# The final norm taken by halves of a row, its root's table loaded behind the sigmoids, and its output rows written from another queue

## The reference, cut to what matters

```
    gate = jax.nn.sigmoid(rms_norm(x, norm_ple) @ w_ple_gate)
    x = x + gate * (pemb @ w_ple_proj)
    ...
    y_prompt = rms_norm(x_p, final_norm)
    y_sample = rms_norm(x_s, final_norm)

def rms_norm(x, gain):
    xf = xf * lax.rsqrt(jnp.mean(xf * xf, axis=-1, keepdims=True) + EPS)
    return (xf * gain.astype(jnp.float32)).astype(x.dtype)
```

## Time and profile before

| what | value |
|---|---|
| median of three runs | 1063.93 us (1061.81 to 1066.5) |
| profiled execution, its own time | 1061.5 us |
| its span (first to last instruction) | 1059.9 us |
| mean granted TensorE clock | 0.992 of full |
| PE busy | 1030.5 us, 97% of the span |
| DVE, ACT, POOL busy | 300.5, 243.0, 91.5 us |
| DMA, mean over the span | 273 GB/s |

### The profile page before, as it was taken

The page is one execution under the profiler, slowest core; times in us unless marked ns, Lnnn a source line. Parts: engine busy times, 40 slices in busy tenths (PEclk is TensorE's granted clock), DMA queues, the critical chain, the costliest instruction groups (busy, mean ns, idle before and its releaser), DMA issues.

```text
span 1059.9 us, 14325 instructions
## 1 busy us (share of the span) xinstructions
PE 1030.5 (97%) x5734; PEld 524.7 (50%) x5734; DVE 300.5 (28%) x798; ACT 243.0 (23%) x503; POOL 91.5 (9%) x133
## 2 busy tenths in 40 slices
PE   7999999999999999999999999999999999999994
PEld 4468777455666667775543333333333333333342
DVE  2134222655333323121441111111111111132252
ACT  2021211456222242000231411111111111111153
POOL 0020040000232220000000000000000000000100
PEclk9999999999999999999999999999999999999998
DMA  9980496100655688363399999999999999999921
GB/s 324 262 240 2 157 165 195 53 29 1 185 167 165 215 282 224 152 238 119 124 369 396 376 426 426 426 426 430 427 429 426 428 428 426 427 428 425 377 78 32
DMA packets 58359, 288.93 MB, mean 273 GB/s; under 512 B 10211, under 2 KB 14540, under 8 KB 45566
## 3 DMA queue, kind: packets, MB, share of 16 engines
q1 hardware_dynamic: 48414, 259.61, 63.2%
q0 software_dynamic: 9648, 28.43, 9.6%
q10 hardware_dynamic: 240, 0.09, 0.0%
HBM read 277.87 MB, written 19.55 MB: 281 GB/s over the span
## 4 chain that ended last, share of the span: by engine, by line
PE 54%; DMA 8%; DVE 1%; issue 1%; ACT 0%; POOL 0%; SPq 0%; DVEq 0%; POOLq 0%
PE ps L1207 19%; PE ps L608 9%; PE ps L1235 9%; DMA reg_k<-in_w_exp_up_dram 7%; PE ps L1179 4%; PE ps L1104 3%; PE ps L679 2%; PE ps L1192 1%; PE ps L1183 1%; DMA late<-y_rows 1%; PE ps L1223 1%; PE ps L627 1%; PE ps L1075 1%; PE ps L686 1%; DVE x L2285 0%
## 5 line engine op out<-in xcount | busy, mean ns | idle before, releaser
L1207 PE MATMUL ps<-ring,reg_xh 128*64 128x512 f32 x512 | 148.7, 595 | 2.3 <-DMA ring<-in_w_exp_up_dram 0.9
L1207 PE MATMUL ps<-late,reg_xh 128*64 128x512 f32 x336 | 148.6, 595 | 0.7 <-DMA reg_k<-in_w_exp_up_dram 0.7
L1207 PEld LDWEIGHTS ps<-ring,reg_xh 128*64 128x64 f32 x512 | 46.2, 137 | 86.7 <-issue 84.2
L2252 DVE TENSOR_TENSOR reg_xh<-reg_xh,ps 64x512 f32<-64x512 f32 x32 | 22.1, 692 | 230.0 <-ACT reg_xh L1619 230.0
L1619 ACT ACTIVATE reg_xh<-ps 64x512 f32<-64x512 f32 x32 | 34.0, 1064 | 213.5 <-PE ps L1207 213.5
L1207 PE MATMUL ps<-reg_k,reg_xh 128*64 128x512 f32 x176 | 77.8, 595 | 0.0
L2471 POOL DMA_INDIRECT y_rows<-reg_xh,slot_row x29 | 28.3, 976 | 544.3 <-ACT reg_xh L1630 503.3
L917 PE MATMUL ps<-reg_xh,ring 128*128 128x320 f32 x256 | 73.5, 436 | 0.0
L1207 PEld LDWEIGHTS ps<-late,reg_xh 128*64 128x64 f32 x336 | 44.4, 137 | 45.3 <-issue 44.7
L608 PE MATMUL ps<-reg_xh,ring 128*128 128x320 f32 x224 | 60.9, 433 | 0.0
L1179 PE MATMUL ps<-reg_xh 128*64 128x512 f32 x256 | 60.5, 592 | 0.0
(11 more groups left out here) (425 smaller groups left out, 1374.4 us busy)
## 6 DMA issues: line engine op xcount, KB each, us to landing
ring<-in_w_exp_gate_dram SPq DMA_DIRECT2D x21, 2048.0 KB, 19.2
ring<-in_w_in_dram SPq DMA_DIRECT2D x12, 2048.0 KB, 10.5
ring<-in_w_exp_down_dram SPq DMA_DIRECT2D x11, 2048.0 KB, 23.9
ring<-in_w_exp_up_dram SPq DMA_DIRECT2D x11, 2048.0 KB, 23.7
late<-in_w_exp_gate_dram SPq DMA_DIRECT2D x10, 2048.0 KB, 19.8
reg_k<-in_w_exp_up_dram SPq DMA_DIRECT2D x10, 2048.0 KB, 24.2
late<-in_w_exp_up_dram SPq DMA_DIRECT2D x10, 2048.0 KB, 23.2
reg_xh<-in_w_exp_down_dram SPq DMA_DIRECT2D x10, 2048.0 KB, 23.4
```

The lines of the kernel that those rows point to most:

```text
L1207: last = pe.matmul(out[64 * part:64 * part + 64, :], xb[:, k, :], ws_[part][:, k, :], start=(k == 0), stop=(k == KT - 1))
L2252: dve.tensor_tensor(sg.rearrange("p (m q) -> p m q", m=4), sg.rearrange("p (m q) -> p m q", m=4), ps[64:128, 2 + par, :].rearrange("p (q m ...
```

## The change

It does four things.

1. ACT executes a root of a number nobody needs (`stat[:, 1, 1, t]`) right behind the sigmoids of each tile, and then takes the squares in two halves of 512, each of which waits for its half of `x` alone. The two sums go to two columns of `stat`.
2. DVE adds the two sums with two small instructions and, between them, multiplies `x` with `gain_f` by halves into `ysb` (`gained`). After the reciprocal, one `tensor_scalar` multiplies the 1024 channels of `ysb` by it, in place.
3. The three transfers of output rows are issued by SP and no longer by POOL. SP waits for `normalised` ahead of each.
4. The copy of window rows is counted by a semaphore that it shares with the gates' transfers (`gate_out` gets a new name), POOL waits for it inside the block, and `out_done` counts the three output transfers alone (48).

```diff
@@ block.sync, behind the branch
+            for t in range(2):
+                sp.wait_ge(normalised, t + 1)
+                sp.dma_start(y_prompt[0, 128 * t:128 * t + 128, :], ysb[:, t, :]).then_inc(out_done, 16)
+            sp.wait_ge(normalised, 3)
+            sp.dma_start(y_sample.rearrange("a b n -> (a b) n"), ysb[0:64, 2, :]).then_inc(out_done, 16)
@@ block.scalar, for each tile behind its sigmoids
-                act.wait_ge(y_done, 2 * t + 2)
-                act.activation(ysb[0:rows, t, :], x[0:rows, t, :], ACT.Square,
-                               accum_out=stat[0:rows, 4, 0, t:t + 1]).then_inc(sq_done, 1)
+                link(act.activation(stat[:, 4, 2, t:t + 1], stat[:, 1, 1, t:t + 1], ACT.Sqrt))
+                for c in range(2):
+                    act.wait_ge(y_done, 4 * t + c + 1)
+                    act.activation(xn2[0:rows, t, 512 * c:512 * c + 512], x[0:rows, t, 512 * c:512 * c + 512], ACT.Square,
+                                   accum_out=stat[0:rows, 4 - c, 0, t:t + 1]).then_inc(sq_done, 1)
                 act.wait_ge(var_ready, 6 + t)
                 act.activation(stat[:, 4, 2, t:t + 1], stat[:, 4, 1, t:t + 1], ACT.Sqrt).then_inc(rms_ready, 1)
@@ block.vector, for each tile behind the two additions
-                dve.wait_ge(sq_done, 13 + t)
-                dve.tensor_scalar(stat[:, 4, 1, t:t + 1], stat[:, 4, 0, t:t + 1], 1.0 / D, EPS, ALU.mult, ALU.add).then_inc(var_ready, 1)
+
+                def gained(c):
+
+                    dve.wait_ge(y_done, 4 * t + c + 1)
+                    cs = slice(512 * c, 512 * c + 512)
+                    dve.tensor_tensor(ysb[0:rows, t, cs], x[0:rows, t, cs], gain_f[0:rows, cs], ALU.mult).then_inc(y_done, 1)
+
+                dve.wait_ge(sq_done, 13 + 2 * t)
+                link(dve.tensor_scalar(stat[:, 4, 1, t:t + 1], stat[:, 4, 0, t:t + 1], 1.0 / D, EPS, ALU.mult, ALU.add))
+                gained(0)
+                dve.wait_ge(sq_done, 14 + 2 * t)
+                dve.scalar_tensor_tensor(out=stat[0:rows, 4, 1, t:t + 1], in0=stat[0:rows, 3, 0, t:t + 1], scalar=1.0 / D,
+                                         in1=stat[0:rows, 4, 1, t:t + 1], op0=ALU.mult, op1=ALU.add).then_inc(var_ready, 1)
+                gained(1)
                 dve.wait_ge(rms_ready, 6 + t)
                 link(dve.reciprocal(stat[:, 4, 3, t:t + 1], stat[:, 4, 2, t:t + 1]))
-                dve.scalar_tensor_tensor(out=ysb[0:rows, t, :], in0=x[0:rows, t, :], scalar=stat[0:rows, 4, 3, t:t + 1],
-                                         in1=gain_f[0:rows, :], op0=ALU.mult, op1=ALU.mult).then_inc(normalised, 1)
+                dve.wait_ge(y_done, 4 * t + 4)
+                dve.tensor_scalar(ysb[0:rows, t, :], ysb[0:rows, t, :], stat[0:rows, 4, 3, t:t + 1], None, ALU.mult).then_inc(normalised, 1)
@@ block.gpsimd
-            pool.dma_start(wnew[:, 0:PAST - NQ, :], wold[:, NQ:PAST, :]).then_inc(out_done, 16)
+            pool.dma_start(wnew[:, 0:PAST - NQ, :], wold[:, NQ:PAST, :]).then_inc(gates_window_out, 16)
...
             pool.dma_start(gain_f, at(final_norm, 0, [[0, 128], [1, D]])).then_inc(gain_f_in, 16)
-            for t in range(2):
-                pool.wait_ge(normalised, t + 1)
-                pool.dma_start(y_prompt[0, 128 * t:128 * t + 128, :], ysb[:, t, :]).then_inc(out_done, 16)
-            pool.wait_ge(normalised, 3)
-            pool.dma_start(y_sample.rearrange("a b n -> (a b) n"), ysb[0:64, 2, :]).then_inc(out_done, 16)
             pool.wait_ge(v_out, 16)
             pool.wait_ge(kv_out, 16 * 6)
+            pool.wait_ge(gates_window_out, 64)
@@ outputs_stored
-            pool.wait_ge(out_done, 64)
+            pool.wait_ge(out_done, 48)
```

More of the change, by code:

```diff
@@ L341, in build @@
         values_in = [sem(f"values_in{i}") for i in range(2)]
-        tab_out, bias_in, mask_in, gate_out, gate_in = sem("tab_out"), sem("bias_in"), sem("mask_in"), sem("gate_out"), sem("gate_in")
+        tab_out, bias_in, mask_in, gates_window_out, gate_in = sem("tab_out"), sem("bias_in"), sem("mask_in"), sem("gates_window_out"), sem("gate_in")
         kv_out, out_done = sem("kv_out"), sem("out_done")
@@ L2408, in _ @@
                 pool.dma_start(at(gate_rows, br, [[3, NS], [3 * NS, H]]), gates[0:64, 2, H * br:H * br + H],
-                               allow_slow_non_contiguous=True).then_inc(gate_out, 16)
+                               allow_slow_non_contiguous=True).then_inc(gates_window_out, 16)
             filled(pool, ("mid", 1, 1))
@@ L2413, in _ @@
                 pool.dma_start(tz[a:a + COPIES], at(tab, MAXD - 128 - a, [[TABN - 1, COPIES], [COPIES * TABN, H], [1, 256]])).then_inc(bias_in, 16)
-            pool.wait_ge(gate_out, 48)
+            pool.wait_ge(gates_window_out, 48)
             for b in range(NB):
```

## The result

| | before | after |
|---|---|---|
| median of the runs | 1063.65 us (6 runs, 1061.81 to 1066.5) | 1056.78 us (6 runs, 1054.0 to 1060.58) |
| profiled execution | 1061.5 us, span 1059.9 | 1057.44 us, span 1055.7 |
| PE's last matmul ends at | 1044.60 us | 1047.02 us |
| tail: from there to the end of the span | 15.3 us | 8.7 us |

The ratio is 0.993 with a 95% interval of [0.991, 0.995]: 6.9 us less in the medians, where 6.3 were forecast. The two spans differ by 4.2 us only, because in the profiled execution of after PE itself came to its end 2.4 us later. The tail doesn't vary in that way, and so it is the quantity to compare: 6.6 us less. It repeated to 0.01 us in a second profile.

What follows compares the result with a forecast made beforehand. The end was taken to be set by POOL's draining, about 4.8 us after the data landed. 1050.62 + 0.07 + 2.8 + 0.05 = 1053.54 against 1059.88, 6.3 us less; median 1063.93 - 6.3 = 1057.6 us, range 1055.0 to 1061.2.

Steps and rivals of the forecast that it cites:

- the cover: Gate multiplication hiding POOL's drain, from near 1000 us to about 1027; without it the drain costs its 7.36 us again.
- Steps (1) to (4): Sample tile: sigmoids end at 1045.61, second half's sum 1047.04, early table load and root 1047.14, squares by halves 1048.5.
- (5): DVE's small instructions around the first half's weight product: the second small one runs from 1048.8 to 1048.97.
- (6): ACT's root without a load, 1049.0 to 1049.2; second weight product until 1049.7, then reciprocal and gaps to 1049.9.
- (7): Last instruction, `tensor_scalar` over 1024 elements: 0.72 us at the copies' pace, bounds 0.67 and 1.28, ending at 1050.62.
- The upper bound of 4.5: Longest landing in us allowed for SP's output write, from SP's reads of twice the bytes at the launch.
- A slow landing: Rival: SP's output write lands in 3.9 us or more, saving 3.7 to 5.2 us, 1059.5 us; chance 0.10.
- No gain from the queue: Rival: any output write pays the drain's time, so only 1.0 + 0.35 us stay, 1062.6 us; chance 0.10.
- The slower side: Rival: SP's last write takes 20.3 us like its last read, end 11.1 us later, about 1075 us; chance 0.03.

Runs made afterwards that it cites:

- queue_only: Kernel before with only the queue's half: SP issues output rows, window copy counted apart, norm as before; tail 10.03 us, ratio 0.9938.
- pool_late_no_write: Changed kernel, POOL also waits for its last load and the last output row before the block's end, issuing nothing there; tail 13.09 us.
- no_early_root: Changed kernel without the unneeded root, so the root's table is loaded behind the squares; tail 8.65 us against 8.68.

## Why the prediction was right, point by point

**What bounds the kernel.** Right, and it was the heart of it: the end was the end of POOL's DRAIN and not of the data. Taken from behind the last write, it gave back 8.22 - 2.97 = 5.25 us between the row and the end (before against queue_only). What the DRAIN waits for the prediction had half right. It took POOL's for one that waits for transfers, and with a load in flight the end does follow the landing; but pool_late_no_write drained for 6.85 us with nothing in flight. The sum did not hang on it, since either reading has the DRAIN hidden at 1000 us: forecast to be over by 1027, it was over at 1019.1. The statement that 7.36 us would be paid again without the cover was right in kind: the DRAIN took 6.85 us there and 4.4 us of tail came back.

**The computing chain.** Forecast 1.0 us, measured 1.34. Steps (1) to (4) hold to 0.02 us when counted from PE's end: sum of the second half at 2.44 forecast and 2.44 measured, early root's end 2.54 and 2.53, second square's sum 3.9 and 3.89. The forecast that the squares end about where they ended before (3.89 against 4.04), because the load ahead of them eats what the halves bring, is what the rows show, and no_early_root confirms it: without that load they end at 3.20. The step that was mis-sized is (5) and (6): I let each DVE instruction start behind the end of the one before. Three of them start 0.07 us before it: the second small one at 1051.14, where the first product ends at 1050.53 + 0.68 = 1051.21; the second product at 1051.21, where the small one ends at 1051.28; and the reciprocal at 1051.81, where the product ends at 1051.88. These 0.22 us, and gaps and a small instruction (0.145 us) that I had taken 0.1 too long in all, moved the reciprocal from 5.1 to 4.78 behind PE. (7) was 0.745 us, forecast 0.72: the copies' pace was the right row and L2147's 1.155 the wrong one. The 0.05 in it for the scalar stood on no row, and no run takes it apart. The Trainium skill's rule ("VectorE: DVE Perf Modes", "The perf-mode tier table (the rule you actually need)") that a float32 `tensor_scalar` in SBUF runs at twice the pace of a `tensor_tensor` is borne out by this contiguous instruction: 0.745 us for 1024 elements, where a product of 512 took 0.68.

**The queue.** Issue behind the row 0.03 us, forecast 0.07; landing 2.9, forecast 2.8; final wait 0.04, forecast 0.05. The upper bound of 4.5 was far off: this SP write landed in 2.9 us where the same write from POOL had taken 2.8. SP's DRAIN took 0.38 us behind its issue and did not wait for the write, as forecast.

**The rivals.** A slow landing: refuted by 2.9. No gain from the queue: refuted by queue_only. The rule behind it in the Trainium skill ("Trainium Kernel Development and Optimization", "Key Constraints") speaks of issue time alone; here the choice of the queue was worth 5.25 us, of which 0.39 is the time from the row to the issue; the transfer itself was no faster (2.9 against 2.8 us). The slower side (a landing of 20 us) did not come near. That the early root does less than the change's name says was in the prediction only as "nearly all hidden"; for the row it does nothing, and the prediction didn't ask what the norm would take without it.

**The size.** 6.3 us forecast, 6.6 in the tail: the row came 0.31 us earlier than forecast, the issue 0.04, and the landing took 0.09 longer. The medians' 6.9 has an interval of about 2.3 us on either side, which holds both. The stated range, 1055.0 to 1061.2, is not the "2.5 us on either side" that the prediction gives for it but 2.6 below and 3.6 above; it holds the 1056.78 either way.

## What to carry to other kernels

Look at what the engines do behind the last busy instruction: the rows at the line that ends the block can hold microseconds that busy time and the chain of waits don't show. Let POOL come to that line early, with the last write issued from another engine's queue; earlier writes can stay. And price a step that is hidden by what it holds up: the table load of 1.28 us moved ahead of the squares brought the root only 0.22 us sooner, because the squares then waited for it, and not even that reached the row.

## What the runs showed that I had not expected

POOL's DRAIN took 6.85 us with all its transfers landed 37 us before, 7.36 to 7.58 behind a write whether of 4, 256 or 512 KB, ended 3.44 us behind the landing of a load still in flight, and fell to 3.75 us when 120 more transfers had been issued in mid-kernel. At the launch, before any transfer, it is 0.18 us. On SP the same instruction took 0.38 us behind its own write, and 0.013 in the kernel before. DVE started an instruction up to 0.08 us before the one ahead of it ended where no result had to be waited for.
